# A two-layer mixer and expert kernel: the second mixer's norm made tile by tile, and the last expert's output handed on in smaller pieces

## The reference, cut to what matters

```python
for layer in range(2):
    xn = rmsnorm(h, norm_mix_g[layer])
    h = h + (even_mixer if layer == 0 else odd_mixer)(xn, ...)
    h = h + cross_attn(rmsnorm(h, norm_xa_g[layer]), ...)
    h = h + hier_moe(rmsnorm(h, norm_ffn_g[layer]), ...)

def rmsnorm(x, g):
    return x * rsqrt(mean(x * x, -1) + 1e-6) * g
def hier_moe(t, ...):          # 16 experts of width 256, two for each token
    hid = silu(t @ w1[e]) * (t @ w3[e])
    return sum(gate[e] * (hid @ w2[e]) for e in two_chosen(t))
```

## Time and profile before

| | us |
|---|---|
| median of 3 runs | 1407.99 (1407.66 to 1408.3) |
| profiled execution, its own time | 1410.12 |
| profiled execution, span from first to last instruction | 1408.3 |
| PE busy | 1204.4 (86%) |
| DVE busy | 576.6 (41%) |
| ACT busy | 478.3 (34%) |
| POOL busy | 372.4 (26%) |

### The profile page before, as it was taken

How to read it: one execution, slowest core, us unless ns; L and a number is a source line. 1 busy time by engine, 2 the same in 40 slices (tenths; PEclk the granted TensorE clock), 3 DMA queues, 4 the chain that set the end, 5 groups by cost and what they waited for, 6 DMA issues and landing times.

```text
span 1408.3 us, 14320 instructions
## 1 busy us (share of the span) xinstructions
PE 1204.4 (86%) x5059; PEld 868.5 (62%) x5059; DVE 576.6 (41%) x1060; ACT 478.3 (34%) x964; POOL 372.4 (26%) x320
## 2 busy tenths in 40 slices
PE   5998999998994999991899699848998994999991
PEld 2557686887673555551797578526887673555551
DVE  5853713304224444444302970761305224444443
ACT  3433255346330222223302433432446230222230
POOL 2032513541243000102414446121340243001102
PEclk9999999999995999996869899978999985999995
DMA  8514113651038799964011311100311037799915
GB/s 247 179 69 94 51 51 117 220 198 60 0 127 325 268 369 377 372 220 150 21 58 60 119 60 61 60 0 0 120 60 60 0 150 313 276 377 369 375 80 209
DMA packets 77830, 222.69 MB, mean 158 GB/s; under 512 B 21900, under 2 KB 22840, under 8 KB 65464
## 3 DMA queue, kind: packets, MB, share of 16 engines
q1 hardware_dynamic: 65680, 183.37, 35.4%
q0 software_dynamic: 10400, 37.79, 7.4%
q10 hardware_dynamic: 1688, 0.71, 0.2%
HBM read 188.95 MB, written 31.46 MB: 157 GB/s over the span
## 4 chain that ended last, share of the span: by engine, by line
PE 72%; DVE 13%; ACT 6%; issue 5%; DMA 2%; POOL 2%; SPq 1%; POOLq 0%; DVEq 0%; ACTq 0%
PE bank L739 33%; PE bank L1028 16%; PE bank L1052 7%; PE bank L773 4%; PE bank L966 2%; PE bank L1090 2%; PE bank L1173 1%; DMA E<-ybuf,pos 1%; DVE E2r L1957 1%; PE bank L910 1%; ACT E2r L1452 1%; SPq L554 1%; PE bank L957 1%; DVE E L2032 1%; POOL E L667 1%
## 5 line engine op out<-in xcount | busy, mean ns | idle before, releaser
L605 POOL TENSOR_TENSOR wlo<-W,whi 128x512 fp32r<-128x512 f32 x176 | 248.9, 1422 | 523.6 <-ACT whi L1222 523.2
L1222 ACT ACTIVATE whi<-W 128x512 fp32r<-128x512 f32 x176 | 109.4, 635 | 338.4 <-PE bank L739 333.4
L739 PE MATMUL bank<-whi,xTr 128*128 128x512 f32 x480 | 189.6, 395 | 10.7 <-DVE E L2032 8.5
L739 PE MATMUL bank<-wlo,xTr 128*128 128x512 f32 x416 | 163.3, 393 | 0.0
L1028 PE MATMUL bank<-W,E 128*128 128x512 f32 x256 | 118.0, 615 | 3.4 <-DVE E L1939 3.4
L1028 PE MATMUL bank<-E 128*128 128x512 f32 x256 | 112.4, 592 | 0.0
L739 PEld LDWEIGHTS bank<-whi,xTr 128*128 128x128 f32 x480 | 91.1, 190 | 30.7 <-issue 11.9
L1052 PE MATMUL bank<-whi,E2r 128*128 128x512 f32 x256 | 91.0, 417 | 12.7 <-DVE E2r L1957 12.3
L739 PEld LDWEIGHTS bank<-wlo,xTr 128*128 128x128 f32 x416 | 79.1, 190 | 16.4 <-issue 0.2
L1028 PEld LDWEIGHTS bank<-W,E 128*128 128x128 f32 x256 | 50.1, 197 | 62.5 <-issue 56.8
L1028 PEld LDWEIGHTS bank<-E 128*128 128x128 f32 x256 | 48.5, 190 | 54.9 <-issue 53.6
(11 more groups left out here) (428 smaller groups left out, 2235.9 us busy)
## 6 DMA issues: line engine op xcount, KB each, us to landing
E<-in_moe_w SPq DMA_DIRECT2D x48, 1024.0 KB, 8.8
W<-in_moe_w SPq DMA_DIRECT2D x32, 1024.0 KB, 7.4
xT<-in_moe_w SPq DMA_DIRECT2D x16, 1024.0 KB, 10.3
ybuf<-E SPq DMA_DIRECT2D x32, 512.0 KB, 4.3
W<-in_od_w_in SPq DMA_DIRECT2D x7, 2048.0 KB, 8.4
W<-in_w_mem_kv SPq DMA_DIRECT2D x4, 2048.0 KB, 8.3
W<-in_xa_wq SPq DMA_DIRECT2D x4, 2048.0 KB, 8.1
ybuf<-memV POOLq DMA_DIRECT2D x8, 1024.0 KB, 12.5
```

The source lines that it names most:

```text
L605: pool.tensor_tensor(wlo[s_ % RING][:, :], slot(name)[:, k, :], whi[s_ % RING][:, :].bitcast(F32), ALU.subtract).then_inc(S["w_lo"], 1)
L739: ins = pe.matmul(bank(u + t)[:, :], a, b, start=(k == 0 and n == 0), stop=(k == KT - 1 and n == 2))
L1222: act.activation(whi[s_ % RING][:, :], slot(name)[:, k, :], ACT.Copy).then_inc(S["w_hi"], 1)
```

## The change

Four edits. First, DVE no longer makes the second mixer's norm for all tiles after the combining, but for tile t-1 after tile t was combined (`norm_tile`): mean, reciprocal and scaling for one tile; ACT takes one square root for each tile (`tile_root`), in its list just ahead of the squares of the next tile. The weights' high parts that stood between squares and root now stand ahead of both. Second, PE's 32 transposes go tile by tile, eight into the eight banks for each tile, and all banks are filled with the last tile. Third, the last item of the last quad is stored in two halves of 512 columns, each as its bank is copied; this is in both layers. Fourth, each of the eight gathers has a semaphore of its own, and DVE waits for one gather ahead of each of its instructions; this too is in both layers.

```diff
@@ -161,11 +161,12 @@
         stat_ready hmean_ready hstd_ready mean_ready std_ready xn_ready s5_args s5_exp s5_sin s5_bb s5_pp s5_w s5_t memk_norm
         ln_mean ln_sq vh_ready ws_masked s5_scan s5_x ya_hi gated ya_lo hd_sq max_ready probs mo_probs
         a_step d_step p_step qk_ready d_norm ml_args ml_act ml_rows diag_ready dt_ready conv_in hh_sq hh_rstd hh_ready
-        spare_rows out_stored xs_stored onehots_ready slots_ready table_ready gate_args gate_exp msum_ready""".split()
+        spare_rows out_stored xs_stored tile_mean tile_std y_gathered00 y_gathered01 y_gathered10 y_gathered11 y_gathered20 y_gathered21 y_gathered30 y_gathered31
+        onehots_ready slots_ready table_ready gate_args gate_exp msum_ready""".split()
         S = {n: sem(n) for n in names}
         per_layer = """w13_0 w13_1 w13_2 w13_3 w2_0 w2_1 w2_2 w2_3 w2_hi w2_lo ht_hi
         idx_ready pool_waited xg_in0 xg_in1 xt_filled xt_ready hid_filled silu_ready hid_ready ht_filled ht_ready
-        y_filled0 y_filled1 y_ready0 y_ready1 y_stored0 y_stored1 y_gathered0 y_gathered1 y_gathered2 y_gathered3
+        y_filled0 y_filled1 y_ready0 y_ready1 y_stored0 y_stored1
         h_half h_combined""".split()
         M = [{n: sem(f"{n}_{l}") for n in per_layer} for l in range(2)]
 
@@ -529,7 +530,12 @@
                     if l == 0 and j < 2:
                         sp.wait_ge(m["hid_filled"], last_quad * SLOTS + (j + 1))
                         load_panel(first_of_layer1 + j, slot_is_free=True)
-                    store(last_quad, j)
+                    if j < SLOTS - 1:
+                        store(last_quad, j)
+                for half in range(2):
+                    sp.wait_ge(m[f"y_ready{half}"], last_quad * SLOTS + SLOTS)
+                    sp.dma_start(ybuf[l][bass.ds(last_quad * (SLOTS * P) + (SLOTS - 1) * P, P), half * 512:(half + 1) * 512],
+                                 yo[1][:, half * 512:(half + 1) * 512]).then_inc(m["y_stored1"], 16)
 
 
             sp.dma_start(memtok, A["mem"][0].rearrange("(a p) d -> p a d", p=P)).then_inc(S["mem_in"], 16)
@@ -661,12 +667,12 @@
                         gather(q, j)
 
                 for par in range(2):
-                    wait_alone(m[f"y_stored{par}"], last_quad * (8 * SLOTS) + 8 * SLOTS)
+                    wait_alone(m[f"y_stored{par}"], last_quad * (8 * SLOTS) + 8 * SLOTS + 16 * par)
                 for t in range(TT):
                     for j in range(2):
                         pool.indirect_dma_start(Yg[j][:, t, :], None, ybuf[l],
                                                 bass.IndirectOffsetOnAxis(ap=pos[:, j, t:t + 1], axis=0))\
-                            .then_inc(m[f"y_gathered{t}"], 16)
+                            .then_inc(S[f"y_gathered{t}{j}"], 16)
             low_parts("out00", "out01")
 
 
@@ -706,6 +712,16 @@
 
                 u0 = first[name]
                 src = xn if name == "mix_norm1" else h
+                if name == "mix_norm1":
+                    for k in range(KT):
+                        claim(pe, u0 + k)
+                    for t in range(TT):
+                        pe.wait_ge(S["xn_ready"], MT + TT + t + 1)
+                        for k in range(KT):
+                            ins = pe.transpose(bank(u0 + k)[:, t * P:(t + 1) * P], src[:, t, k * P:(k + 1) * P], ident[:])
+                            if t == TT - 1:
+                                fill(ins, u0 + k)
+                    return
                 for k in range(KT):
                     claim(pe, u0 + k)
                     for t in range(TT):
@@ -1231,11 +1247,19 @@
 
                 a_(act.activation(spare[:, 0:1], ones[:, 0:1], func))
 
+            def tile_root(name, t):
+
+                n = NORMS[name]
+                act.wait_ge(S["tile_mean"], t + 1)
+                act.activation(std[:, n, t:t + 1], ssq[:, n, t:t + 1], ACT.Sqrt).then_inc(S["tile_std"], 1)
+
             def squares(name):
 
                 n = NORMS[name]
                 for t in range(TT):
                     h_is_ready(name, t)
+                    if name == "mix_norm1" and t:
+                        tile_root(name, t - 1)
                     if name == "mix_norm0":
                         dst = memV[:, t % MT, :]
                         if t >= MT:
@@ -1246,17 +1270,19 @@
 
             def root(name):
                 n = NORMS[name]
-                act.wait_ge(S["mean_ready"], n + 1)
+                act.wait_ge(S["mean_ready"], n + 1 - (n > NORMS["mix_norm1"]))
                 act.activation(std[:, n, :], ssq[:, n, :], ACT.Sqrt).then_inc(S["std_ready"], 1)
 
             def norm(name, between=None):
+                if between:
+                    between()
                 if name != "mix_norm0" and "xa" not in name:
                     table(ACT.Sqrt)
                     squares(name)
-                if between:
-                    between()
-                if name != "mix_norm0" and "xa" not in name:
+                if "ffn" in name:
                     root(name)
+                if name == "mix_norm1":
+                    tile_root(name, TT - 1)
                 gain, lo = {"mix": ("norm_mix_g", 0), "xa_": ("norm_xa_g", 0), "ffn": ("norm_ffn_g", 0)}[name[0:3]]
                 lo = 8 * int(name[-1])
                 if first[name] in two_parts:
@@ -1590,13 +1616,18 @@
                 rstd_of(ssq[:, n, :], std[:, n, :], rstd[:, n, :], D, "mean_ready", "std_ready",
                         "rstd_ready" if name in LAST_ADD else None)
 
+            def norm_tile(name, t):
+
+                n = NORMS[name]
+                c = slice(t, t + 1)
+                dve.wait_ge(S["stat_ready"], 2 + 4 * (n - 1) + t + 1)
+                rstd_of(ssq[:, n, c], std[:, n, c], rstd[:, n, c], D, "tile_mean", "tile_std")
+                ts(xn[:, t, :], h[:, t, :], rstd[:, n, c], None, ALU.mult).then_inc(S["xn_ready"], 1)
+
             def norm(name):
                 n = NORMS[name]
-                if name != "mix_norm0" and "xa" not in name:
+                if "ffn" in name:
                     rstd_of_tokens(name)
-                if name == "mix_norm1":
-                    for t in range(TT):
-                        ts(xn[:, t, :], h[:, t, :], rstd[:, n, t:t + 1], None, ALU.mult).then_inc(S["xn_ready"], 1)
                 gain = {"mix": "norm_mix_g", "xa_": "norm_xa_g", "ffn": "norm_ffn_g"}[name[0:3]]
                 lo = 8 * int(name[-1])
                 if first[name] in two_parts:
@@ -1982,12 +2013,16 @@
                 quad(last_quad, False)
 
                 for t in range(TT):
-                    dve.wait_ge(m[f"y_gathered{t}"], 32)
                     for j in range(2):
+                        dve.wait_ge(S[f"y_gathered{t}{j}"], 16 * (l + 1))
                         if j:
                             dve.wait_ge(m["h_half"], t + 1)
                         stt(h[:, t, :], Yg[j][:, t, :], gate[:, j, t:t + 1], h[:, t, :], ALU.mult, ALU.add)\
                             .then_inc(m["h_combined" if j else "h_half"], 1)
+                    if l == 0 and t:
+                        norm_tile("mix_norm1", t - 1)
+                if l == 0:
+                    norm_tile("mix_norm1", TT - 1)
 
             attention(0)
             experts(0)
```

## The result

The changed kernel takes 1412.05 us (median of 8 runs, 1409.86 to 1413.31), the kernel before 1408.11 in the runs beside it. The medians stand 3.9 us apart; the ratio over all runs is 1.0023 with an interval of 1.0014 to 1.0032, that is 2.0 to 4.5 us slower, 3.2 in the middle. The forecast was 1401.8, faster, and is wrong.

A forecast was written before the change was run, and what follows sets the result against it. Matmuls on PE bound the kernel; gains come only where the chain leaves PE. Front 5.2 less clock 0.6 plus layer 1's end 1.6 gives 6.2 us, 1407.99 to 1401.8, range 1399.2 to 1404.9.

The forecast's parts named there:

- The clash on DVE: Second mixer's norm: POOL's low parts slow each DVE instruction they meet by about 1.0 us; last scaling 672.5, unhindered 671.0.
- 1.3 us per wait: Second mixer's norm, pessimistic bound: full waits of DVE for POOL and a clash for the means, tile 3 scaled at 673.7.
- lie in its idle time: ACT ahead of the second mixer's norm: four weight conversions moved into ACT's idle time take 2.08 us from the chain.
- The first matmul then hangs on bank 0: Start of the second mixer's gemm: first matmul waits for bank 0's parts, 2.3 us after the last scaling, at 674.8.
- The clock: First gemm panel of the second mixer: 1.3 us at the low clock, 0.6 us lost, bounds 0 and 2.5 us.
- The tail: Layer 1's end: store gives 0.6, one instruction fewer 1.3, 0.3 lost; sum 1.6 us, bounds 0.8 and 2.0.
- The store in halves: Last store of the experts, both layers: everything behind it starts 0.6 us earlier, bounds nothing and 0.65.
- the 0.3 us for the rest: Layer 1's end: tile 0's output store starts about 1.9 us earlier and shares DMA engines with gathers longer, 0.3 lost.
- DVE is the bound: Rival, second mixer's front: DVE's rounds, clashes and handovers eat the tiles' gain; 3.6 us faster, 1404.4; chance 0.10.
- The gemm starts cold: Rival, first gemm panel: low clock lasts through more of it, 2.5 us lost; 4.3 us faster, 1403.7; chance 0.14.
- Nothing measurable: Rival, whole change: halves and single waits give nothing, front DVE-bound with cold start; 0.9 us faster, 1407.1; chance 0.05.
- Slower: Rival, first gemm panel: PE's work so broken up that the clock stays at 0.50 throughout; 1421; chance 0.03.

The follow-up runs named there:

- e5: Changed kernel, with POOL waiting for the last scaled tile and the first gemm claiming bank by bank: ratio 0.9949 to the kernel before, 1400.99 us.
- e2: Changed kernel, with POOL making the panel's low parts only when the last tile is scaled: ratio 0.9965 to the kernel before.
- e3: Changed kernel, with the first gemm claiming each of its four banks just before using it: ratio 0.9991 to the kernel before.
- e11: Changed kernel, with ACT's four weight conversions back between the squares and the last root: ratio 0.9993 to the kernel before.
- e7: Changed kernel, with tiles 0 to 2 transposed twice to keep PE busy: ratio 1.0017 to the kernel before.
- e8: Kernel before, with only the last store split in halves: ratio 1.0002 to the kernel before.
- e10: Changed kernel with late POOL low parts and bank-by-bank claims, DVE again waiting for both gathers of a tile: ratio 0.9967 to the kernel before.
- e9: Kernel before, with only a semaphore and a wait for each gather: ratio 1.0003 to the kernel before.
- e4: Changed kernel, with the 32 transposes bank by bank again behind the last scaling, norm still by tile: ratio 1.0008 to the kernel before.
- e1: Changed kernel, with norm, ACT's list and transposes as before, halves and single waits kept: ratio 1.0001 to the kernel before.

## Why the prediction was wrong

What bounds the kernel, and where, was right: all that moved beyond the scatter of the middle is in the front of the second mixer and in the tail. Front (to the panel's end) and tail of the traces give, against before, +2.5 - 0.8 = 1.7 us for the changed kernel, -7.4 - 0.4 for e5, -3.5 - 0.7 for e2, -1.8 - 0.1 for e3; the runs say 3.2, -7.2, -4.9 and -1.3, each with about 1.5 us of uncertainty. The sum had forecast 4.6 us of gain in the front; it became 2.5 us of loss. Three steps hold these 7.1 us: 2.7, 2.3 and 2.1.

1. *The clash on DVE* was seen, and mis-sized. The step gave it 1.5 us on the last scaling: "about 1.0 us for each DVE instruction that meets one of POOL's", taking turns as in the earlier trace rows. POOL took no turns: four low parts ran in 4.92 us (4.96 in e2, behind the last scaling), and one DVE instruction stood behind all of them. e2 takes 4.9 us off. (Without any clash the forecast had the last scaling at 671.0, 26.7 us behind the last copy, and e2 has it at 26.0; so it came 2.7 us later than forecast and not 3.4.) The bound that I set, 1.3 us per wait, was too tight as well. e11 shows what set it off: the step "lie in its idle time" counted the 2.08 us that ACT saves; that POOL's work moves with them was seen, but not that it could hold DVE for its whole length.

2. *"The first matmul then hangs on bank 0"* is the step that was wrong in kind. It hangs on banks 0 to 3: `split_gemm` claims four banks before its first matmul, and in the ring they are the banks of the norm's first four transposes. Before, the claims were covered by 5.12 us of transposes; the change took away the cover. The gemm began 4.6 us behind the last scaling, not 2.3. e3 shows it by the claims alone. The line was in the function that I priced; I followed `x_ready`, the wait with the data, and not the wait for space.

3. *The clock.* 0.6 us were counted, and 2.7 were lost (24.71 against 22.04), a little more than the bound of 2.5. Its mechanism was right, with one link missing: that transposes raise the clock was read rightly from the earlier trace rows and e7 repeats it; the pause of step 2 undoes it. With the pause gone e3 has 22.45 and e5 22.04 us. The Trainium skill's rule in "TensorE: Matmul & The Clock Gate", Part 4, that transposes don't engage the high level, is not what these fp32 transposes do: 13 of them stand alone ahead of the rise at 666.2 in e7.

The runs weigh the steps. Without the first (e2) the kernel takes 1403.8 us, inside the forecast's range; without the second and what it does to the clock (e3) it takes 1408.0, outside. That e5, without all three, comes to 1401.0 and so near the forecast of 1401.8 is luck: it has no clash on DVE and no low clock in the panel, so 7.4 us in the front instead of 4.6, and in the tail 0.4 instead of 1.6.

*The tail* was forecast at 1.6 us, and the trace has 0.8. The store in halves gave 0.7 where 0.6 was said, and the one instruction left behind the landing gave its 1.3. The term that was too small is the 0.3 us for the rest: from the first gather's issue to the last landing the changed kernel takes 17.9 us, before it was 16.7. All traces with single waits have 17.7 to 18.8 there, the three with pairs (before, e8, e10) 16.7 to 17.0. Slower issues are one part: the eight take 11.0 us instead of 9.85 in the changed kernel, and 12.2 in e9. They are not all of it: in e5, e7 and e11 the eight take 10.0 and the last rows still come at 18.1 to 18.3. The output stores, which start 2.0 us earlier, are the candidate that the prediction names; no run tests them. In layer 0 the store gave 0.35 instead of 0.6. Neither edit alone moves the time by what can be measured.

Of the rivals, "DVE is the bound" and "The gemm starts cold" both came true, together. The sum had priced each with the other's part intact, 1404.4 and 1403.7. "Nothing measurable" had both, and 0.8 us for the tail as measured, and came to a gain of 0.9 us; the trace has a loss of 1.7. The 2.6 us between them are the claims for the most part, 2.3, which no rival had. "Slower" is what happened, but not by its mechanism: the clock was low for 5.8 us of the panel and not all through it. What the prediction held against that rival was misread: the trace of before does show dense work at the low level for longer than 5.5 us. From 706 to 730 PE is busy without a break with 0.50 granted, on narrow matmuls (128x8, L1090) and then on the first of the next panel.

*What stays open.* Why POOL took turns with DVE in the earlier trace rows and in the norm of before, and none here. In the four traces without turns (the changed kernel, e3, e4, e7) the instruction held up had begun 0.17 to 0.22 us ahead of POOL's first. In the norm of before, e1, e8 and e9 POOL's four had begun first, and two of the scalings beside them took 1.75 us each, in turns with low parts of 1.71. So the order may decide, but it isn't enough: at 792.8 in the changed kernel a DVE instruction over 128x2048 values (L2046) began 0.67 us ahead of three low parts and took 2.29 us, the least that it takes in any trace. No run varies the order alone. And the median of the changed kernel is 2.1 us above its profiled execution, and e2 gains 8.2 us on it over the runs where the traces show 6.0 at the panel's end: how far the cold start or the clock elsewhere takes part in that no trace here shows.

## What to carry to other kernels

When a stretch of work is shortened, go through every wait that it covered, the waits for space first: here four banks had to be empty, and nobody saw it while 29 transposes ran. A step moved into idle time is not free if it releases work of another engine: ask where that engine's new work falls, and where the two engines hold each other up, as POOL and DVE here, put it behind the path (e2: one wait, 8 us over the runs). And a pause of PE just ahead of a gemm can be paid twice, in waiting and in the clock: 2.2 and 2.3 us in e3.

## What the runs showed of the hardware

- One DVE instruction of 1.28 us (two inputs of 1024 values in SBUF) took 6.22 us beside four POOL subtractions that ran unhindered in 4.92 us; a scaling of 0.75 us took 5.65 in the same place (e4, e7). The Trainium skill's page "SBUF — State Buffer", Who interferes with whom, has an exclusive lock for the whole instruction; here the DVE instruction stood behind four of them.
- POOL's issue of an indirect DMA takes 0.94 us. One that begins while a combining instruction is running on DVE ends 0.80 to 0.82 us behind the end of that instruction, up to 1.99 us after it began (72 of 72 in the fourteen traces); a combining instruction that begins behind the issue doesn't lengthen it.
- The granted clock rose during transposes alone (666.2 in e7) and fell again in a pause of 3.1 us ahead of the gemm; the gemm then ran some 6 us at 0.50.
